# A hybrid encoder step on one core: the expert stage's first loads move into routing, and its first block is ordered anew

## The reference, cut to what matters

```python
logits = (t @ rw + rb).astype(F32)
top_v, top_i = lax.top_k(logits, TOP_K)            # 4 of 32 experts
gate = jax.nn.softmax(top_v, axis=-1)
...
gu = jnp.einsum('nmd,ndf->nmf', xs.reshape(NB, M, D), w1[block_e]) + b1[block_e][:, None]
g_ = jnp.minimum(gu[..., :D_FF], SWIGLU_LIMIT)
up = jnp.clip(gu[..., D_FF:], -SWIGLU_LIMIT, SWIGLU_LIMIT)
act = (up + 1.0) * g_ * jax.nn.sigmoid(SWIGLU_ALPHA * g_)
y = jnp.einsum('nmf,nfd->nmd', act, w2[block_e]) + b2[block_e][:, None]
...
x = LN2(alpha*x + MoE(x) + sigmoid(x Wg + bg) * (p[i] Wp))
```

## Time and profile before

| | |
|---|---|
| Runs of the kernel before | 2686.47, 2686.9, 2694.5 us |
| The profiled execution | 2690.0 us, span 2688.3 us |
| TensorE matmul busy | 2472.5 us, 92% |
| TensorE weight load busy | 2218.1 us, 83% |
| DVE, ACT, POOL busy | 1587.5, 1346.4, 647.1 us |
| Mean granted clock of TensorE | 0.964 |
| DMA | 468.08 MB, mean 174 GB/s |

### The profile page before, as it was taken

The page is one execution under the profiler, slowest core; times in us unless marked ns, Lnnn a source line. Parts: engine busy times, 40 slices in busy tenths (PEclk is TensorE's granted clock), DMA queues, the critical chain, the costliest instruction groups (busy, mean ns, idle before and its releaser), DMA issues. The chain is left out here.

```text
span 2688.3 us, 40408 instructions
## 1 busy us (share of the span) xinstructions
PE 2472.5 (92%) x14988; PEld 2218.1 (83%) x14988; DVE 1587.5 (59%) x2520; ACT 1346.4 (50%) x2119; POOL 647.1 (24%) x491
## 2 busy tenths in 40 slices
PE   7999999998888999999989888699999999999991
PEld 7988797887657999999978567589898998989990
DVE  4656421118658544445434376588887888777774
ACT  4666321126435534334332222387787778777762
POOL 1000200005101011010103204234444444543433
PEclk9999999999989999999999899799999999999995
DMA  8321232202585565565533312689898998988864
GB/s 253 81 67 41 91 116 79 86 28 110 177 267 138 132 171 136 127 156 141 141 109 142 127 51 69 203 262 296 275 298 274 293 286 276 293 259 277 275 193 168
DMA packets 389434, 468.08 MB, mean 174 GB/s; under 512 B 17471, under 2 KB 312603, under 8 KB 389312
## 3 DMA queue, kind: packets, MB, share of 16 engines
q1 hardware_dynamic: 367213, 395.82, 47.0%
q0 software_dynamic: 17760, 60.34, 8.8%
q10 hardware_dynamic: 4338, 10.23, 1.0%
HBM read 397.63 MB, written 68.71 MB: 173 GB/s over the span
## 5 line engine op out<-in xcount | busy, mean ns | idle before, releaser
L3371 PE MATMUL banks<-slot_rowsT,expert_w_high 128*128 128x288 f32 (+2 forms) x2048 | 552.1, 352 | 0.0
L3374 PE MATMUL banks<-slot_rowsT,expert_w_low 128*128 128x144 f32 (+2 forms) x2048 | 489.6, 239 | 0.0
L3374 PEld LDWEIGHTS banks<-slot_rowsT,expert_w_low 128*128 128x128 f32 x2048 | 394.9, 193 | 1.3
L3371 PEld LDWEIGHTS banks<-slot_rowsT,expert_w_high 128*128 128x128 f32 x2048 | 388.3, 190 | 1.4
L3418 ACT CAST expert_w_high<-expert_w 128x2048 fp32r<-128x2048 f32 x128 | 237.9, 1908 | 19.9 <-DMA expert_w<-in_exp_w 19.9
L3477 DVE TENSOR_TENSOR expert_w_low<-expert_w,expert_w_high 128x2048 fp32r<-128x2048 f32 x96 | 216.7, 2284 | 30.8 <-ACT expert_w_high L3418 30.8
L2214 PE MATMUL banks<-xT_chunk_high,w_gates_high 128*128 128x384 f32 x576 | 193.1, 335 | 4.5 <-DVE xT_chunk_low L2286 4.5
L3298 POOL TENSOR_TENSOR expert_w_low<-expert_w,expert_w_high 128x2048 fp32r<-128x2048 f32 x32 | 146.9, 4590 | 198.7 <-ACT expert_w_high L3418 198.7
L2215 PE MATMUL banks<-xT_chunk_low,w_gates_high 128*128 128x384 f32 x576 | 192.9, 335 | 0.0
L2216 PE MATMUL banks<-xT_chunk_high,w_gates_low 128*128 128x384 f32 x576 | 192.9, 335 | 0.0
L3518 DVE TENSOR_TENSOR expert_w_low<-expert_w,expert_w_high 128x1024 fp32r<-128x1024 f32 x128 | 156.8, 1225 | 54.7 <-ACT expert_w_high L3447 54.7
(11 more groups left out here) (528 smaller groups left out, 6197.0 us busy)
## 6 DMA issues: line engine op xcount, KB each, us to landing
expert_w<-in_exp_w SPq DMA_DIRECT2D x126, 1024.0 KB, 7.8
expert_w<-in_exp_w SPq DMA_DIRECT2D x32, 2048.0 KB, 9.6
w_gates<-in_w_in SPq DMA_DIRECT2D x72, 512.0 KB, 4.4
cached_k<-in_cache_sb_k SPq DMA_DIRECT2D x16, 1024.0 KB, 10.4
cached_v<-in_cache_sb_v SPq DMA_DIRECT2D x16, 1024.0 KB, 10.0
w_stream<-in_w_in SPq DMA_DIRECT2D x48, 256.0 KB, 4.2
w_proj<-in_w_pa SPq DMA_DIRECT2D x24, 512.0 KB, 5.1
w_stream<-in_w_in SPq DMA_DIRECT2D x16, 512.0 KB, 5.2
```

The source lines that it names most:

```text
L3371: nc.tensor.matmul(out[:, 0:2 * SLOTS].rearrange("p (a s) -> p a s", a=2)[:, :, 0:width], hi, xgT[:, par, k, :, 0:width], start=(place == ...
L3374: last = nc.tensor.matmul(out[:, 0:width], lo, xgT[:, par, k, 0, 0:width], start=False, stop=(place == DT - 1), skip_group_check=True)
```

## The change

What it does, in the order of the program:

- `xT` becomes `g.rows`, one tensor that stays allocated through the expert stage. The w1 buffer and `xg` lie in it. A class `FirstBlock` names parts of it for block 0's rows (`first_xg`, `first_rest`, inside the memory of w1's second pair) and owns the semaphores shared by routing and experts.
- `set_control` loses the part on all blocks. A new `experts_of_blocks` after unit 5 finds the expert of each block with one block to a partition, and TensorE turns that column after unit 7; the rest of `set_control` runs after unit 9.
- POOL's scatters no longer wait for the weights' split. SP loads the table after the rows of unit 14, DVE casts it after unit 13, TensorE turns it after unit 14, and `keep_table` follows there.
- At the end of routing POOL gathers block 0's rows and SP loads pieces 0 and 1 of its w1, both once `xT` has been split for the last unit. The wait for the residual writes moves from ACT to POOL in the expert stage.
- In the expert stage block 0's transposes use four banks (0, 1, 6, 7); SP loads w1's second pair when they are done, w2 when that pair has landed. The cast and subtraction of w1's first piece are cut in halves. In block 0 ACT and DVE treat hidden pieces 0 and 1 and the casts of w1's pieces 2 and 3 ahead of the split of w2; their loops start at block 2.

```diff
+class FirstBlock:
+    def __init__(self, sem, g):
+        rows = g.rows[:]
+        self.w1 = rows[:, 0:8 * D].rearrange("p (c k a n) -> p c k a n", c=2, k=DT, a=2)
+        self.xg, self.first_xg, self.first_rest = rows[:, 8 * D:], rows[:, 4 * D:5 * D], rows[:, 5 * D:5 * D + D // 2]
...
@@ stage_route, SP
-            for n in range(R, len(units)):
+            for n in range(R, TABLE_AT + 2):
                 load_rows(n)
             sp.wait_ge(scattered, 16 * NT * TOPK)
             sp.dma_start(table_rows.bitcast(I32), g.table_d.rearrange("(b s) o -> b (s o)", s=SLOTS)
                          ).then_inc(table_in, 16)
+            for n in range(TABLE_AT + 2, len(units)):
+                load_rows(n)
+            sp.wait_ge(ctl_ready, 1)
+            sp.wait_ge(x_split, len(units))
+            sp.wait_ge(x_high, len(units))
+            e = sp.value_load(g.ctl[0:1, 1:2], min_val=0, max_val=NE - 1)
+            src = g.exp_w1[0][bass.ds(e, 1)].rearrange("o (k p) n -> p (o k) n", p=P)
+            for f, landed in enumerate(g.first.w1_in):
+                for part in range(2):
+                    lo = part * FF + f * P
+                    sp.dma_start(g.first.w1[:, 0, :, part, f * P:(f + 1) * P], src[:, :, lo:lo + P]
+                                 ).then_inc(landed, 16)
@@ stage_route, POOL
-            pool.wait_ge(w_split, 2 * PIECES)
...
+            pool.wait_ge(tables_kept, 1)
+            pool.tensor_copy(g.idx[:], g.table[:, 0, 0:2]).then_inc(g.first.idx_ready, 1)
+            pool.wait_ge(g.first.idx_ready, 1)
+            pool.wait_ge(x_split, len(units))
+            pool.wait_ge(x_high, len(units))
+            pool.indirect_dma_start(
+                out=g.first.first_xg, out_offset=None, in_=g.x1_d,
...
@@ stage_route, ACT
-            for s in res_out:
-                act.wait_ge(s, 16 * (2 * NT // R))
@@ stage_route, DVE
+            def experts_of_blocks():
+                block_id = place_of[:, 0:1]
+                dve.wait_ge(table_clear, 1)
+                link(nc.vector.scalar_tensor_tensor(out=key, in0=order, scalar=NFEW - 0.5, in1=eid[:],
+                                                    op0=ALU.is_lt, op1=ALU.mult))
+                link(nc.vector.scalar_tensor_tensor(out=key, in0=order, scalar=block_id, in1=key,
+                                                    op0=ALU.is_equal, op1=ALU.mult))
+                link(nc.vector.tensor_reduce(of_block[:, 0:1], key, AX_X, ALU.add))
+                link(nc.vector.tensor_scalar(key, upto, block_id, None, ALU.is_le))
+                link(nc.vector.tensor_reduce(of_block[:, 1:2], key, AX_X, ALU.add))
+                nc.vector.scalar_tensor_tensor(out=of_block[:, 0:1], in0=of_block[:, 1:2], scalar=float(NE - 1),
+                                               in1=of_block[:, 0:1], op0=ALU.min, op1=ALU.add
+                                               ).then_inc(experts_found, 1)
...
                 if n == 5:
+                    experts_of_blocks()
+                if n == NT:
                     set_control()
-                if n == 2 * NT - 2:
+                if n == TABLE_AT:
                     cast_table()
-            keep_table()
+                if n == TABLE_AT + 1:
+                    keep_table()
@@ stage_experts, SP
-            for f, landed in enumerate((w1_first_in, w1_in[0])):
-                if f:
-                    sp.wait_ge(w1_first_in, 32)
-                for part in range(2):
-                    lo = part * FF + f * P
-                    sp.dma_start(w1[:, 0, :, part, f * P:(f + 1) * P], src[:, :, lo:lo + P]).then_inc(landed, 16)
-
-            sp.wait_ge(xg_in, 32)
+            sp.wait_ge(t_ready, 4)
             load_w1(e, 1)
+            sp.wait_ge(w1_in[1], 32)
             load_w2(e)
@@ stage_experts, POOL
-            gather(0)
-            pool.nop().then_inc(y_left, 1)
-
-            pool.wait_ge(t_ready, 4)
             gather(1)
             w1_last_low_part(0)
+            for s in g.first.res_out:
+                pool.wait_ge(s, 16 * (2 * NT // 3))
+            pool.nop().then_inc(y_left, 1)
@@ stage_experts, ACT (DVE alike: hidden(0), w1_low_part(2), hidden(1), low_parts(0), low_parts(1))
+                if first:
+                    for f in range(2):
+                        hidden(n, par, f)
+                        w1_high_part(2 + f, 0)
+                    for f in range(2):
+                        high_parts(n, par, ahead, f)
+                for f in range(2 if first else 0, FT):
+                    hidden(n, par, f)
+                    high_parts(n, par, ahead, f)
...
-            each_block(act, step)
+            for par in range(2):
+                step(par, par, 2, par == 0)
+            each_block(act, step, 1)
```

229 lines of the change are left out of this document (142 added, 87 removed).

## The result

The changed kernel takes 2682.99 us (median of 16 runs, 2674.56 to 2688.2), the kernel before, run beside it, 2688.13 (16 runs). The ratio is 0.9972, 95% interval 0.9963 to 0.998. That is 7.5 us faster (5.4 to 9.9), where 19.2 were forecast; the two medians lie 5.1 apart. Repeated unchanged on another chip it gave 0.9976 (0.9966 to 0.9986). The profiled execution took 2679.33 us, span 2677.6. That is 10.7 less than the span of before, and a short one among its runs.

What follows compares the result with a forecast made beforehand. TensorE bounds the expert stage proper, so an earlier block 1 ends the program earlier; four stretches ahead aren't TensorE-bound. 7.1 + 1.9 + 10.7 + 0 - 0.5 = 19.2 us, giving 2667.7 against the median 2686.9; range 2659 to 2682.

Steps and rivals of the forecast that it cites:

- Block list, 7.1: Routing: moving the expert-count calculation out of DVE's unit loop gains 7.1 us (bounds 3 and 8.5).
- R2: Rival: routing's gain is lost to late second-half weights or tenth unit's product; 3 of 7.1 remain, 2671.8 us; chance 0.10.
- Scatters and table: Routing: scatters begin some 30 us earlier, about 1607; table cast about 1667, with about 6 us of cover.
- R3: Rival: slow early scatters delay the table and TensorE loses 25 us or more after unit 14, 2695 us; chance 0.03.
- Loads in routing: End of routing: block 0's gather and weight loads, issued about 1682, land by 1695, before wanted at 1697.3; hidden.
- R5: Rival: the moved loads don't come early; the expert stage finds its data 4 to 7 us later, 2673 us; chance 0.10.
- Border 1.9, start 10.7: Routing's end shrinks from 3.9 to 2.0 us, gain 1.9; stage start to first weight matmul from 14.8 to 4.1, gain 10.7.
- Block 0: First expert block, from its first matmul: 38.3 us against 38.2 before, for other reasons; gain 0 (bounds -5 and +6).
- R1: Rival: block 0 gets 6 us shorter, with w1 at 7.5 us, no hold and full clock, 2661.7 us; chance 0.17.
- As long as the 31 blocks after it keep their pace: Expert stage: premise that block 1 beginning earlier ends the program earlier by as much, closing stage untouched.
- R4: Rival: the later blocks' pace shifts; 0.6 us a block over 31 blocks gives 2687, 0.3 gives 2677; chance 0.10.
- At the end of the program one more set of semaphores is cleared with a barrier: loss 0.5: Program end: clearing one more set of semaphores with a barrier costs 0.5 us.

Runs made afterwards that it cites:

- b2: Kernel after, but ACT and DVE treat block 0 in the old order of casts, ahead of the first activations; 2686.76 us, ratio 0.998.
- d2: Kernel after with DVE's wait for the norm vectors moved from ahead of the first moments to the first scale; 2681.19 us, ratio 0.9963.
- d3: Kernel after with the norm-vector wait moved to the first scale and POOL awaiting block 0's gathers before leaving routing; 2681.8 us, ratio 0.9964.
- b1: Kernel before with the block list by partitions alone; 2683.79 us, ratio 0.9977.
- e1: Kernel after, but POOL issues the gather for block n+2 before waiting for block n-1's scatter to land; 2673.01 us, ratio 0.9939.
- d4: Kernel after, POOL awaiting block 0's gathers before leaving routing, block 0's w2 load issued right behind w1's second pair; 2681.97 us, one run.

## Why the prediction was wrong

The mechanism was right up to the first weight matmul, and the forecast missed behind it. Means over the profiles of the changed kernel whose gathers stand as in the change (eleven; ten for block 0, without `b2`), against the two of before:

| | forecast | first profile | mean |
|---|---|---|---|
| first weight matmul earlier | 19.7 | 18.4 | 18.3 |
| block 0 | 0 | -2.0 | -2.5 |
| blocks 1 to 30 | 0 | -0.2 | -3.1 |
| from block 31 on | -0.5 | -5.5 | -5.4 |
| sum | 19.2 | 10.7 | 7.3 |

The last row is the mean of nine, without `d2` and `d3`, which change the closing stage. The last column's sum agrees with the 7.5 us of the ratio.

The prediction named 929 us from block 1 to the end as a sign that it would be wrong. It is 934.7 in the changed kernel's profile (929.0 before): the sign came true.

- *Block list, 7.1:* right. `b1` has 7.3 us at the first weight matmul (1719.6 to 1712.4). In the changed kernel's profile the last write is 5.9 earlier. The wait of 6.69 is gone; TensorE's waits for DVE in routing come to 7.5 us instead of 12.7. R2 didn't occur.
- *Scatters and table:* right. They run from 1607 and TensorE doesn't wait for the table: its list of waits from 1590 to the border has only DVE's products, 7.5 us in four. R3 is excluded.
- *Loads in routing:* right, issued at 1683.1 and 1683.4 against 1682; the gathers landed at 1691.4 (7.0 us after the second issue at 1684.4), the loads by 1696.1, before the stage asked for them. R5 is excluded.
- *Border 1.9, start 10.7:* 2.16 us from the last issue's end to the stage's start instead of 3.89, so 1.7; and 4.03 us to the first weight matmul where 4.1 was worked out.
- *Block 0:* a term mis-sized. w1's second pair took 11.3 us from its issue to the cast (1702.13 to 1713.41) and not 9.6, the median of the single 2 MB load; that median is of another transfer, one DMA of 2 MB and not two of 1 MB. The trace of before had the same pair: SP issued it at 1716.43 and ACT cast it at 1728.49, 12.1 us. This line of SP's timeline of before was there to be read:

```profile
1716.43 2.47 SPq L3229 DMA_DIRECT2D expert_w<-in_exp_w  x2
```

Piece 2 started at 15.0 after the first matmul (forecast 13.4), the addition of piece 3 ended at 31.7 (29.8), the products took 8.5 as said. These 1.9 us are the whole difference between 38.3 and 40.2, but the late pair explains 1.1 of them at most: DVE's held subtraction ended at 23.4 (forecast 22.3). From there I had gone on in rounds of DVE, and the trace goes over TensorE. Piece 3 started at 24.6, behind DVE's row parts, and ACT waited 1.73 us for its low sum (1733.01). In the first 3.7 of its 5.5 us (1727.3 to 1731.0) the mean granted clock was 0.56, close to the lower level of 1.2 GHz; ahead of it TensorE had stood idle for 2.09 us. The products then came 0.46 us apart, at full clock 0.25.

The hold of DVE's subtraction came as forecast: 3.61 us at 1722.50 beside POOL's 4.56 of 1720.47, done 1.1 us after POOL, and 1.21 for the next one. The Trainium skill's page "SBUF — State Buffer", section "SBUF: two separate sides", counts such a pair of operations among those that exclude each other, and the trace agrees. R1 didn't occur: "each wait is followed by another", as the prediction had it. The wait that I had put directly before piece 3 shows up as 2.09 us before the turn of rows ahead of it, whose bank waits for DVE's row parts behind the held subtraction.
- *"As long as the 31 blocks after it keep their pace":* this premise failed, as R4 had it, but with a wrong picture of how. R4 priced it as a constant shift per block, with a chance of 0.10. What happens are single late gathers, waits of up to 5.7 us in 6 to 12 of 30 blocks (that block of `d2` is 8.4 longer than its neighbours); the profile of before had them too, 3.4 us in 8 blocks in its view of waits, and the forecast made nothing of them. `e1` shows that the place of the gather decides it. That they cost more in the changed kernel rests on 11 profiles against 2 (3 with `b1`): 7.6 against 4.6 us of waits for gathers, 846.0 against 842.9 us of blocks, with ranges that overlap. Why the change makes them more is not settled.
- *"At the end of the program one more set of semaphores is cleared with a barrier: loss 0.5":* this step failed by size and by kind. The clear costs about the 0.5; POOL's drain ahead of it costs 4.8. No row of before could have told its size: there the drain took 1.78 us, and only the changed kernel's trace has 6.60. But "the closing stage is untouched" was assumed without a rival about the far end of the stage. Why the drain is longer stays open, as told above.
- The conversion to the median took 3.1 us off, from three runs; with 16 runs the profile of before lay 1.9 over its median. That alone would have made the forecast 2668.9 instead of 2667.7, and doesn't matter beside the rest. The range ended at 2682.0, 1 us short.

## What to carry to other kernels

A start moved forward is paid out only if everything behind it keeps its slack: before counting on "the same pace", list the waits of the steady part and ask for each small one what it stands behind; a transfer queued behind another's landing, with a margin below the spread of landing times, turns up as rare large waits. Where a change issues an engine's DMAs in another stage than before, compare the drains at every later border in both traces: here one of them grew by 4.8 us, 940 us behind the DMAs that were moved. Take a load's time from the same transfer in the trace of before and not from a median over others. And when a wait on a landing guards one buffer, put it directly ahead of that buffer's next use and issue what doesn't need it first.

## What was not expected of the hardware

- POOL's DRAIN ahead of the barriers at the two ends of the expert stage takes 1.8 to 10.3 us in these kernels, the same within 15 ns in two profiles of one kernel. At the end of routing, with no gather under way, it took 2.992 us after 36 indirect DMAs and 3.155 after 38, 0.08 us for each. At the end of the expert stage it took 1.780 or 6.598 us, as told above, cause open.
- POOL is held by DVE as well as the other way round. In `d2` its copy of 128x2 numbers took 2.32 us instead of 0.18: it began beside a subtraction of weights on DVE (1769.27, two in 4.50 us) and ended with the first of them. In all 20 profiles 116 of 623 such copies took over 0.5 us, and every one of them ended 0.04 to 0.05 us after a subtraction of weights did. The issues of POOL's gathers behave alike: 534 of 1231 took over 1.3 us (the others 0.94 to 1.29), and every one ended 0.82 to 0.89 us after such a subtraction.
- The two loads of 1 MB of w1's second pair took 11.0 to 12.3 us from the first issue to the cast that waits for both, in all 20 profiles, with w2's 2 MB beside them (the kernel before, `b1`, `d4`) or without.
